# A state-space mixer's output products with operands swapped, and its output turned through DRAM instead of on VectorE

## The chip, the cores and the metric

The kernel runs on one core of a Trainium2 chip. The metric is the time of one execution on the device in microseconds, the median of the runs. The engines are TensorE (PE; PEld is its weight load), VectorE (DVE), ScalarE (ACT), GpSimd (POOL) and SyncE (SP); SP, ACT and POOL also issue transfers, which 16 DMA engines carry out.

## What is computed

A decoder trunk of two layers over 256 tokens of width 2048 in float32. Layer 0 mixes tokens with a gated spatial unit, layer 1 with an S5 state-space layer; each layer then has a SwiGLU block and a gated per-layer embedding. The change lies in layer 1's mixer:

```python
u = (h @ w_in).astype(f32)                       # 256 x 2048
lam_bar = jnp.exp(lam * dt)                      # 128 groups x 64 complex states
bu = lax.complex(...)                            # group input (16 channels) into 64 states
_, s = lax.associative_scan(_lin_combine, (a, bu), axis=1)
y = (jnp.einsum('blgp,gcp->blgc', jnp.real(s), c_re.astype(f32))
     - jnp.einsum('blgp,gcp->blgc', jnp.imag(s), c_im.astype(f32)))
y = y.reshape(bsz, seq, S5_WIDTH) + d.astype(f32) * u
g = jax.nn.gelu(y).astype(h.dtype)
val, gate = jnp.split(g @ w_out, 2, axis=-1)
return val * jax.nn.sigmoid(gate)
```

## The kernel before

All large products go through a stream of 792 weight tiles of 256 x 512 numbers (`ORDER`, tile index t). SP loads tile t into a ring of four buffers (`RAW`), ACT rounds it to its high part (`WHI`, L717), DVE subtracts to get the low part (`WLO`, L976), and PE multiplies with twelve matmuls of 512 columns (high x high, high x low, low x high: L1385 to L1387). ACT's high part of tile t waits until PE has finished tile t-4. The order on every engine is written out by hand: on ACT and DVE, `until(W0 + g)` brings the splitting up to tile W0 + g + 2, and then come the other works of step g. W0 is the first tile of stage `win` (product with `s5_w_in`, 32 tiles); then comes `out1` (product with `s5_w_out`).

Between these tiles lies the S5 core. The sequence of 256 tokens is cut into 32 chunks (NC) of 8 tokens (T). A duo d (8 of them) is 16 groups of 16 channels, two blocks of 128 channels. `turn_u` and `u_chunks` bring u out of token order into `UC` (PE, then DVE, L1282); ACT stores it to the DRAM tensor `ud` and loads it back with channels and in-chunk positions on the partitions as `UP`. `into_states` (L1606, after tile `INTO_AT[d]`) gives the states' inputs, `scan` on DVE (from L1292) runs over the chunks, and `out_of_states` (after tile `OUT_AT[d]`) adds the products with the in-chunk taps `TKK` (L1624) and of the states `SD` with the tables `TD` (L1632). Before `out_of_states` PE waits for the scan, for the tables and for the next `UC`.

The result lies in PSUM with the chunks on the partitions, four strips of 32. `take_y` (ACT, L906) applies GELU and writes `YP`; `turn_y` (DVE, L1315) transposes it in blocks of 32 x 32 into `YG`, which has channels on the partitions; `y_high` (ACT, L913) and `y_low` (DVE, L1320) split that into the high and low parts of the operand `OP` for `out1`. `out1` goes through its first three columns at once: `EARLY` lists them as (column, depth). Column 0 waits for `y_ready` of duo j at depth j; its depths 0 to 7 stand at tiles W0 + 32, 34, 36, 38, 44, 47, 50 and 53.

```python
OUT_AT = [W0 + 8 * (d // 2) + 17 + 2 * (d % 2) for d in range(DUOS - 2)] + [W0 + 42, W0 + 43]
OUT_BANK = [6] * (DUOS - 2) + [4, 4]
Y_AT = [t + 2 for t in OUT_AT]
```

On ACT `take_y(d)` stands at step `OUT_AT[d] + 1` and `y_high(d)` at `Y_AT[d]`; on DVE `turn_y(d)` at `OUT_AT[d] + 2` and `y_low(d)` at `Y_AT[d] + 1`.

Of the kernel before, what the change touches and what calls it, by code (L numbers as in the profile page):

```python
# [6 lines left out]
F32 = mybir.dt.float32  # L7
F32R = mybir.dt.float32r
I32 = mybir.dt.int32
ACT = mybir.ActivationFunctionType  # L10
# [3 lines left out]
P = 128  # L14
# [15 lines left out]
CH = 16  # L30
ST = 64
T = 8
NC = TOK // T
PAIRS = GROUPS // 2
QP = 4
GB = 8
DUOS = KB // 2
DP = 2 * QP
# [34 lines left out]
def end(stage, n):  # L73
    return INDEX[stage, n, DEPTH_OF[stage] - 1] + 1
# [76 lines left out]
W0 = start("win")  # L151
UT_AT = [W0 + 8 * n + 8 for n in range(NT)]
INTO_AT = [W0 + 8 * (d // 2) + 14 + d % 2 for d in range(DUOS)]
OUT_AT = [W0 + 8 * (d // 2) + 17 + 2 * (d % 2) for d in range(DUOS - 2)] + [W0 + 42, W0 + 43]

OUT_BANK = [6] * (DUOS - 2) + [4, 4]
Y_AT = [t + 2 for t in OUT_AT]
DSET = [0, 1, 2, 0, 1, 0, 1, 0]


# [15 lines left out]
def trunk(nc, x, p, norm_mix, norm_ffn, norm_ple, norm_final, gm_w_in, gm_ln_g, gm_ln_b, gm_w_s, gm_b_s,  # L176
# [3 lines left out]
    with ctx:  # L180
        def sem(name):
            return ctx.enter_context(nc.semaphore(name))

        KBYTE = 1024
# [5 lines left out]
        def place(name, shape, dt=F32, at=None):  # L190
            size = 4
            for s in shape[1:]:
                size *= s
            if at is None:
                at = top[0]
                top[0] += (size + 31) // 32 * 32
                assert top[0] <= base + ARENA, name
            return nc.alloc_sbuf_tensor_at(name, shape, dt, offset=at)
# [7 lines left out]
        s_at = top[0]  # L206
# [77 lines left out]
        TD = [f_view(f"TD{i}", [P, 2, QP, 2, P], 16 + 8 * i) for i in range(2)] + [op_view("TD2", [P, 2, QP, 2, P], 8)]  # L284
        TKK = [f_view(f"TK{i}", [P, 2, GB, P], 32 + 8 * i) for i in range(2)] + [op_view("TK2", [P, 2, GB, P], 16)]
# [4 lines left out]
        SD = [op_view(f"SD{i}", [P, 2, DP, NC], 42 + 2 * i) for i in range(2)]  # L290
        RT = [op_view(f"RT{i}", [P, DP, NC], 46 + i) for i in range(2)]
        UC = place("UC", [P, QB, T, NC], at=pt_at)
        UP = [op_view(f"UP{i}", [P, QB, GB, NC], 24 + 4 * i) for i in range(2)]

        YP = place("YP", [P, 2, T, 2, CH], at=s_at)
        YG = place("YG", [P, 2, T, NC], at=s_at + 2 * KBYTE)
        VAL = f_view("VAL", [P, 2, NW], 0)


# [3 lines left out]
        PS = ctx.enter_context(nc.psum_tensor("PS", [P, 8, NW], F32))  # L303
# [3 lines left out]
        tabk = nc.dram_tensor("tabk", (KB, P, T * P), F32).ap()  # L307
        tabe = nc.dram_tensor("tabe", (2, P, PAIRS * NC), F32).ap()
        ud = nc.dram_tensor("ud", (NT, QB, P, T * NC), F32).ap()

        raw_in = [sem(f"raw_in{s}") for s in range(RING)]
        hi_ready = sem("hi_ready")
# [68 lines left out]
        sd_ready = sem("sd_ready")  # L381
        out_of = sem("out_of")
        yp_ready = sem("yp_ready")
        yg_ready = sem("yg_ready")
        y_hi = sem("y_hi")
        y_ready = sem("y_ready")
        g_in = sem("g_in")
# [317 lines left out]
        def _(act):  # L705
            A_ = nc.scalar
# [193 lines left out]

            def take_y(d):
                act.wait_ge(out_of, d + 1)
                if d:
                    act.wait_ge(yg_ready, d)
                for g in range(2):
                    last = A_.activation(YP[:, :, :, g, :].rearrange("p b i c -> p b c i"),  # L906
                                         PS[:, OUT_BANK[d] + g, 0:2 * P].rearrange("p (b c i) -> p b c i", b=2, i=T),
                                         ACT.Gelu_apprx_tanh)
                last.then_inc(yp_ready, 1)

            def y_high(d):
                act.wait_ge(yg_ready, d + 1)
                A_.activation(OP[:, 2 * d:2 * d + 2, 0:TOK].rearrange("p b (k i) -> p b k i", i=T),  # L913
                              YG[:, :, :, :].rearrange("p b i k -> p b k i"), ACT.Copy).then_inc(y_hi, 1)

            for g in range(5, 62):
                until(W0 + g)
                for n in range(NT):
                    if W0 + g == end("win", n):
                        if n:  # L920
                            act.wait_ge(ut_done, 2 * n)
                        take("win", n, in_z, ACT.Copy)
                    if W0 + g == UT_AT[n] + 2:
                        store_u(n)
                    if W0 + g == UT_AT[n] + 4:
                        spread_u(n)
                for d in range(DUOS):
                    if W0 + g == Y_AT[d]:
                        y_high(d)
                    if W0 + g == OUT_AT[d] + 1:  # L930
                        take_y(d)
                if W0 + g == end("out1", 0):
                    act.wait_ge(in_done, DUOS)
                    take("out1", 0, lambda th: VAL[:, th, :], ACT.Copy, scaled=False)
                if W0 + g == end("out1", 1):
                    take("out1", 1, in_s, ACT.Sigmoid, scaled=False)
                if W0 + g == end("out1", 2):
                    act.wait_ge(z_ready, Z_COUNT["out1", 1])
                    take("out1", 2, lambda th: VAL[:, th, :], ACT.Copy, scaled=False)
# [25 lines left out]
        def _(dve):  # L965
            step = Chain(dve, dve_chain)
            V_ = nc.vector
# [57 lines left out]
            for i in range(4):  # L1025
                r = slice(32 * i, 32 * i + 32)
                last = V_.tensor_tensor(IDENT[r, r], IOTA[r, 1, :], IOTA[r, 2, :], ALU.is_equal)
# [142 lines left out]
            for n in (1, 2, 4):  # L1170
                pause()
                last = lambda ri: LP[:, ri, n:n + 1, :].to_broadcast([P, n, PAIRS])
# [18 lines left out]
            for n in range(NT):  # L1191
                f = slice(NW * n, NW * n + NW)
                for th in range(2):
                    last = V_.tensor_scalar(V[:, th, f], V[:, th, f], MV[:, th, 0:1], LNR[:, th, :], ALU.subtract, ALU.mult)  # L1194
# [4 lines left out]
            for n in range(NT):  # L1199
# [5 lines left out]
                for th in range(2):  # L1205
                    for m in range(QB):
                        h = QB * n + m
                        c = slice(P * m, P * m + P)
# [99 lines left out]
                V_.tensor_tensor(SD[d % 2][:, 1, :, 1:NC], part(CV, 1), part(CA, 0), ALU.add).then_inc(sd_ready, 1)  # L1308
                dve.wait_ge(sd_ready, d + 1)

            def turn_y(d):
                dve.wait_ge(yp_ready, d + 1)
                if d:
                    dve.wait_ge(y_ready, d)
                V_.transpose(YG[:, :, :, :].rearrange("p b i k -> p (b i k)"),  # L1315
                             YP[:, :, :, :, :].rearrange("p b i g c -> p (b i g c)")).then_inc(yg_ready, 1)

            def y_low(d):
                dve.wait_ge(y_hi, d + 1)
                V_.tensor_tensor(OP[:, 2 * d:2 * d + 2, TOK:2 * TOK].rearrange("p b (k i) -> p b k i", i=T),  # L1320
                                 YG[:, :, :, :].rearrange("p b i k -> p b k i"),
                                 OP[:, 2 * d:2 * d + 2, 0:TOK].bitcast(F32).rearrange("p b (k i) -> p b k i", i=T),
                                 ALU.subtract).then_inc(y_ready, 1)

            dve.wait_ge(core_ready, 1)
            for g in range(7, 62):
                until(W0 + g)
                for n in range(NT):
                    if W0 + g == UT_AT[n] + 1:
                        u_chunks(n)  # L1330
                for d in range(DUOS):
                    if W0 + g == INTO_AT[d] + 1:
                        scan(d)
                    if W0 + g == Y_AT[d] + 1:
                        y_low(d)
                    if W0 + g == OUT_AT[d] + 2:
                        turn_y(d)
                if W0 + g == end("out1", 1):
                    gated("out1", 1, VAL[:, :, :])
            quad_of("out1", 0, 2)  # L1340
# [25 lines left out]
            f = slice(3 * NW, D)  # L1366
# [6 lines left out]
        def _(pe):  # L1373
# [236 lines left out]
            def out_of_states(d):  # L1610
                n, i, tab = d // 2, d % 2, DSET[d]
                pe.wait_ge(td_in[tab], 32 * (DSET[:d].count(tab) + 1))
                pe.wait_ge(sd_ready, d + 1)
                if d:
                    pe.wait_ge(yp_ready, d)
                pe.wait_ge(uc_ready, 2 * min(n + 2, NT))
                if OUT_BANK[d] == 4:
                    pe.wait_ge(inc_free, DUOS)
                bank = OUT_BANK[d]
                for bl in range(2):  # L1620
                    f = slice(P * bl, P * bl + P)
                    for g in range(2):
                        for q in range(QP):
                            T_.matmul(PS[NC * q:NC * q + NC, bank + g, f], UP[n % 2][:, 2 * i + bl, 2 * q + g, :],  # L1624
                                      TKK[tab][:, bl, 2 * q + g, :], start=(bl == 0), stop=False, skip_group_check=True)
                for bl in range(2):
                    f = slice(P * bl, P * bl + P)
                    for ri in range(2):
                        for q in range(QP):
                            for g in range(2):  # L1630
                                half = slice(ST * g, ST * g + ST)
                                last = T_.matmul(PS[NC * q:NC * q + NC, bank + g, f], SD[i][half, ri, QP * bl + q, :],  # L1632
                                                 TD[tab][half, bl, q, ri, :], start=False, stop=(ri == 1), skip_group_check=True)
                last.then_inc(out_of, 1)

            for t in range(W0, INDEX["out1", 2, 7] + 1):
# [55 lines left out]
```

## Time and profile before

| | |
|---|---|
| time, median of 3 runs (lowest to highest) | 2365.84 us (2365.3 to 2366.28) |
| profiled execution, its own time | 2365.84 us |
| its span, first to last instruction | 2364.1 us |
| mean granted clock of PE | 0.990 |
| busy: PE, DVE, ACT, POOL | 97%, 57%, 44%, 20% |
| weight tiles moved by DMA, mean | 206 GB/s |
| stage of the S5 core | about 1236 to 1390 us |

The page gives each engine's busy time and the chain of work that ended last. As PE is busy nearly all the time, its idle times, its own work and its clock are what makes the length of the kernel. The granted clock is given as a share: 1.00 is 2.4 GHz, 0.50 is 1.2 GHz. Durations of single matmuls overlap, since PE works them in a pipeline: the pace is seen from a burst's length divided by its count.

### The profile page before, as it was taken

The numbers are of one execution on the slowest core, as the hardware profiler recorded it, in microseconds if no ns is written. First come the engines' busy times: TensorE is split into PE (matmuls) and PEld (weight loads), VectorE is DVE, ScalarE is ACT, GpSimd is POOL, SyncE is SP. The second block draws the span as 40 slices with busy tenths as digits, with TensorE's granted clock in tenths as the row PEclk, the third lists the DMA queues.
The fourth block names the chain that finished last, engine by engine and source line by source line (L and its number), as shares of the span: only waits on it lengthen the run. The fifth ranks groups of instructions, "written<-read, shape, count | busy, mean of one in ns | idle before, by whom it ended". The sixth has DMA issues, their size and how long they took to land.

```text
span 2364.1 us, 29152 instructions
## 1 busy us (share of the span) xinstructions
PE 2301.6 (97%) x11853; PEld 1904.2 (81%) x11853; DVE 1336.5 (57%) x1402; ACT 1034.3 (44%) x1252; POOL 474.8 (20%) x438
## 2 busy tenths in 40 slices
PE   5989999999999999999998999999999999999997
PEld 4868888888888888888887788888888888888886
DVE  4786655554555555555656665545445445445565
ACT  3534444444444444444543344444443344444443
POOL 1067304554666355300000000000000000000001
PEclk8999999999999999999999999999999999999999
DMA  6545667766667667666877966566655566665553
GB/s 215 174 152 177 189 194 228 230 216 215 224 219 240 213 217 223 207 214 212 272 245 252 303 212 187 189 192 193 188 187 193 192 193 190 189 190 188 187 205 134
DMA packets 276551, 487.03 MB, mean 206 GB/s; under 512 B 52049, under 2 KB 56545, under 8 KB 276033
## 3 DMA queue, kind: packets, MB, share of 16 engines
q1 hardware_dynamic: 256752, 477.42, 62.6%
q10 hardware_dynamic: 18896, 4.26, 0.8%
q0 software_dynamic: 768, 3.48, 0.4%
q8 instruction: 94, 1.54, 0.3%
q14 instruction: 41, 0.33, 0.0%
HBM read 453.65 MB, written 31.46 MB: 205 GB/s over the span
## 4 chain that ended last, share of the span: by engine, by line
PE 95%; DVE 3%; issue 1%; DMA 1%; ACT 0%; ACTq 0%; SPq 0%; DVEq 0%
PE PS L1385 30%; PE PS L1387 30%; PE PS L1386 30%; PE PS L1414 2%; DVE WLO L976 1%; PE PS L1494 1%; DVE V L1194 1%; PE PS L1632 0%; PE PS L1624 0%; PE PS L1504 0%; PE PS L1606 0%; DMA TE<-tabe 0%; PE PS L1469 0%; DVE OP L995 0%; DVE STAT L1007 0%
## 5 line engine op out<-in xcount | busy, mean ns | idle before, releaser
L976 DVE TENSOR_TENSOR WLO<-RAW,WHI 128x1024 fp32r<-128x1024 f32 x792 | 1038.0, 1314 | 933.0 <-ACT WHI L717 930.9
L1385 PE MATMUL PS<-WHI,OP 128*128 128x512 f32 x3136 | 1235.1, 394 | 27.3 <-DVE WLO L976 27.3
L717 ACT ACTIVATE WHI<-RAW 128x1024 fp32r<-128x1024 f32 x792 | 839.3, 1062 | 941.2 <-PE PS L1387 926.3
L1387 PE MATMUL PS<-WHI,OP 128*128 128x512 f32 x3136 | 1224.0, 390 | 0.0
L1386 PE MATMUL PS<-WLO,OP 128*128 128x512 f32 x3136 | 1223.3, 390 | 0.0
L1385 PEld LDWEIGHTS PS<-WHI,OP 128*128 128x128 f32 x3136 | 590.5, 188 | 154.1 <-issue 33.8
L1387 PEld LDWEIGHTS PS<-WHI,OP 128*128 128x128 f32 x3136 | 590.3, 188 | 124.0
L1386 PEld LDWEIGHTS PS<-WLO,OP 128*128 128x128 f32 x3136 | 591.0, 188 | 119.5
L701 POOL TENSOR_TENSOR ON<-X,GF 128x1024 f32<-128x1024 f32 x3 | 9.9, 3308 | 994.5 <-DVE X L1255 994.5
L640 POOL TENSOR_TENSOR TA<-BRAW,FAC 128x64 f32<-128x64 f32 x16 | 7.1, 445 | 367.3 <-DMA BRAW<-in_s_b_im 367.3
L749 ACT ACTIVATE S<-PS,RC 128x512 f32<-128x512 f32 x68 | 43.1, 685 | 61.9 <-PE PS L1387 61.8
L733 ACT ACTIVATE OP<-PS,VEC 128x256 fp32r<-128x256 f32 x96 | 37.7, 475 | 55.8 <-PE PS L1414 55.8
L995 DVE SCALAR_TENSOR_TENSOR OP<-PS,VEC,OP 128x256 fp32r<-128x256 f32 x96 | 39.7, 477 | 24.5 <-ACT OP L733 24.5
L683 POOL COPY RT<-RHO 128x248 f32<-128x248 f32 x8 | 6.2, 786 | 225.1 <-DVE CB L1299 225.1
L728 ACT ACTIVATE OP<-PS 128x512 fp32r<-128x512 f32 x52 | 28.3, 596 | 52.4 <-PE PS L1414 52.4
L1007 DVE BATCH_NORM_STATS2 STAT<-X 128x6 f32<-128x512 f32 x56 | 35.8, 681 | 0.1
L1244 DVE SCALAR_TENSOR_TENSOR Z<-PS,RC,S 128x512 f32<-128x512 f32 x44 | 31.0, 746 | 7.2 <-PE PS L1387 6.9
L845 ACT ACTIVATE EXP<-PS 128x128 f32<-128x128 f32 (+7 forms) x128 | 17.7, 265 | 39.3 <-PE PS L1504 39.3
L659 POOL TENSOR_TENSOR QT<-TA,TB 128x512 f32<-128x512 f32 x16 | 34.5, 2157 | 1.3
L591 POOL TENSOR_TENSOR V<-V,LG 128x1024 f32<-128x1024 f32 x4 | 11.8, 2959 | 109.7 <-DVE V L1194 109.7
L838 ACT ACTIVATE QS<-PS 128x1024 f32<-128x1024 f32 x16 | 16.4, 1026 | 39.0 <-PE PS L1494 39.0
L989 DVE TENSOR_TENSOR OP<-PS,OP 128x512 fp32r<-128x512 f32 x52 | 33.2, 679 | 0.0
(184 smaller groups left out, 998.3 us busy)
## 6 DMA issues: line engine op xcount, KB each, us to landing
RAW<-in_ffn_w SPq DMA_DIRECT2D x528, 512.0 KB, 4.2
RAW<-in_gm_w_in SPq DMA_DIRECT2D x64, 512.0 KB, 4.3
RAW<-in_ple_w_gate SPq DMA_DIRECT2D x64, 512.0 KB, 4.3
RAW<-in_s_w_out SPq DMA_DIRECT2D x64, 512.0 KB, 4.5
RAW<-in_gm_w_out SPq DMA_DIRECT2D x32, 512.0 KB, 4.1
RAW<-in_s_w_in SPq DMA_DIRECT2D x32, 512.0 KB, 4.8
tabq<-QS SPq DMA_DIRECT2D x16, 512.0 KB, 5.3
tabd<-DT SPq DMA_DIRECT2D x16, 512.0 KB, 6.0
```

The lines of the kernel that those rows point to most:

```text
L659: G_.tensor_tensor(QT[:, :, 1, :, :], TA[:, :, :, :], TB[:, :, :, :], ALU.add).then_inc(q_ready, 1)
L717: A_.activation(WHI[:, t % RING, :], RAW[:, t % RING, :], ACT.Copy).then_inc(hi_ready, 1)
L733: last = A_.activation(OP[:, block_ + 2 * h + m, 0:TOK], PS[:, bank + h, TOK * m:TOK * m + TOK], ACT.Identity, scale=VEC[:, row, k:k + 1])
L749: last = A_.activation(dst(th), acc(stage, n)[:, th, :], func, scale=RC[:, RMS[stage], th:th + 1])
L976: V_.tensor_tensor(WLO[:, t % RING, :], RAW[:, t % RING, :], WHI[:, t % RING, :].bitcast(F32), ALU.subtract).then_inc(lo_ready, 1)
L989: V_.tensor_tensor(OP[:, blocks, TOK:2 * TOK], PS[:, bank + h, :].rearrange("p (k t) -> p k t", t=TOK), OP[:, blocks, 0:TOK].bitcast(F32), ...
L995: last = V_.scalar_tensor_tensor(OP[:, b, TOK:2 * TOK], PS[:, bank + h, TOK * m:TOK * m + TOK], VEC[:, row, k:k + 1], OP[:, b, 0:TOK].bitc ...
L1007: last = V_.bn_stats(STAT[:, th, 6 * n:6 * n + 6], src[:, th, NW * n:NW * n + NW])
L1385: T_.matmul(dst[:, th, :], hi, WHI[:, slot, f], start=begin, stop=False)
L1386: T_.matmul(dst[:, th, :], hi, WLO[:, slot, f], start=False, stop=False)
L1387: last = T_.matmul(dst[:, th, :], lo, WHI[:, slot, f], start=False, stop=finish)
L1414: last = T_.transpose(PS[:, bank + m // 2, at:at + P], src, IDENT[:, :])
```

## The change

In `out_of_states` the two operands of each product are swapped: the table becomes the stationary operand (128 columns of weights), `UP` or `SD` the streamed one (32 columns), and the result has channel and in-chunk position on all 128 partitions and the chunks in the free dimension. `take_y` writes it to one of two `YP` buffers and ACT stores it to a new DRAM tensor `yd` (2048 pieces of 128 bytes for each duo); `gather_y`, four steps later on ACT, loads it back with group and channel on the partitions (256 pieces of 1 KB) into one of two `YG` buffers. The transpose `turn_y` on DVE goes. `y_high` and `y_low` stand six tiles later than before. `YP` and `YG` of one parity share their memory. From the third duo on `take_y` waits for the `y_low` of two duos before.

```diff
...
-Y_AT = [t + 2 for t in OUT_AT]
+YG_AT = [t + 5 for t in OUT_AT]
+Y_AT = [t + 8 for t in OUT_AT]
...
-        YP = place("YP", [P, 2, T, 2, CH], at=s_at)
-        YG = place("YG", [P, 2, T, NC], at=s_at + 2 * KBYTE)
+        YP = [place(f"YP{i}", [P, DP, 2, NC], at=s_at + 2 * KBYTE * i) for i in range(2)]
+        YG = [place(f"YG{i}", [P, 2, T, NC], at=s_at + 2 * KBYTE * i) for i in range(2)]
...
+        yd = nc.dram_tensor("yd", (DUOS, 2 * GB, CH, T, NC), F32).ap()
...
-        yg_ready = sem("yg_ready")
+        yd_in = [sem(f"yd_in{i}") for i in range(2)]
+        yg_in = [sem(f"yg_in{i}") for i in range(2)]
...
             def take_y(d):
...
-                if d:
-                    act.wait_ge(yg_ready, d)
+                if d >= 2:
+                    act.wait_ge(y_ready, d - 1)
                 for g in range(2):
-                    last = A_.activation(YP[:, :, :, g, :].rearrange("p b i c -> p b c i"),
-                                         PS[:, OUT_BANK[d] + g, 0:2 * P].rearrange("p (b c i) -> p b c i", b=2, i=T),
+                    last = A_.activation(YP[d % 2][:, :, g, :], PS[:, OUT_BANK[d] + g, 0:DP * NC].rearrange("p (q k) -> p q k", k=NC),
...
                 last.then_inc(yp_ready, 1)
+                act.wait_ge(yp_ready, d + 1)
+                act.dma_start(yd[d].rearrange("g c i k -> (c i) g k"), YP[d % 2][:, :, :, :].rearrange("p q g k -> p (q g) k")).then_inc(yd_in[d % 2], 16)
+
+            def gather_y(d):
+                act.wait_ge(yd_in[d % 2], 16 * (d // 2 + 1))
+                act.dma_start(YG[d % 2][:, :, :, :].rearrange("p b i k -> p b (i k)"),
+                              yd[d].rearrange("(b g) c i k -> (g c) b (i k)", b=2)).then_inc(yg_in[d % 2], 16)
...
             def y_high(d):
-                act.wait_ge(yg_ready, d + 1)
+                act.wait_ge(yg_in[d % 2], 16 * (d // 2 + 1))
...
-                              YG[:, :, :, :].rearrange("p b i k -> p b k i"), ACT.Copy).then_inc(y_hi, 1)
+                              YG[d % 2][:, :, :, :].rearrange("p b i k -> p b k i"), ACT.Copy).then_inc(y_hi, 1)
...
                         y_high(d)
                     if W0 + g == OUT_AT[d] + 1:
                         take_y(d)
+                    if W0 + g == YG_AT[d]:
+                        gather_y(d)
                 if W0 + g == end("out1", 0):
...
-            def turn_y(d):
-                dve.wait_ge(yp_ready, d + 1)
-                if d:
-                    dve.wait_ge(y_ready, d)
-                V_.transpose(YG[:, :, :, :].rearrange("p b i k -> p (b i k)"),
-                             YP[:, :, :, :, :].rearrange("p b i g c -> p (b i g c)")).then_inc(yg_ready, 1)
-
             def y_low(d):
...
-                                 YG[:, :, :, :].rearrange("p b i k -> p b k i"),
+                                 YG[d % 2][:, :, :, :].rearrange("p b i k -> p b k i"),
...
                     if W0 + g == Y_AT[d] + 1:
                         y_low(d)
-                    if W0 + g == OUT_AT[d] + 2:
-                        turn_y(d)
                 if W0 + g == end("out1", 1):
...
                 bank = OUT_BANK[d]
                 for bl in range(2):
-                    f = slice(P * bl, P * bl + P)
-                    for g in range(2):
-                        for q in range(QP):
-                            T_.matmul(PS[NC * q:NC * q + NC, bank + g, f], UP[n % 2][:, 2 * i + bl, 2 * q + g, :],
-                                      TKK[tab][:, bl, 2 * q + g, :], start=(bl == 0), stop=False, skip_group_check=True)
+                    for q in range(QP):
+                        for g in range(2):
+                            at = NC * (QP * bl + q)
+                            T_.matmul(PS[:, bank + g, at:at + NC], TKK[tab][:, bl, 2 * q + g, :], UP[n % 2][:, 2 * i + bl, 2 * q + g, :],
+                                      start=(at == 0), stop=False, skip_group_check=True)
                 for bl in range(2):
-                    f = slice(P * bl, P * bl + P)
-                    for ri in range(2):
-                        for q in range(QP):
+                    for q in range(QP):
+                        for ri in range(2):
                             for g in range(2):
+                                at = NC * (QP * bl + q)
...
-                                last = T_.matmul(PS[NC * q:NC * q + NC, bank + g, f], SD[i][half, ri, QP * bl + q, :],
-                                                 TD[tab][half, bl, q, ri, :], start=False, stop=(ri == 1), skip_group_check=True)
+                                last = T_.matmul(PS[:, bank + g, at:at + NC], TD[tab][half, bl, q, ri, :], SD[i][half, ri, QP * bl + q, :],
+                                                 start=False, stop=(ri == 1), skip_group_check=True)
                 last.then_inc(out_of, 1)
...
```

## Rows read from the trace of the kernel before

**Rows 1.** the page: busy time of PE, and the chain's shares by engine.

```profile
PE 2301.6 (97%) x11853; PEld 1904.2 (81%) x11853; DVE 1336.5 (57%) x1402; ACT 1034.3 (44%) x1252; POOL 474.8 (20%) x438
...
PE 95%; DVE 3%; issue 1%; DMA 1%; ACT 0%; ACTq 0%; SPq 0%; DVEq 0%
```

**Rows 2.** stretches: busy us (count) by engine, granted clock, DMA share, GB/s.

```profile
1258.00:1262.00 4.00, 4.00 (x100) 3.29 (x93) 0.69 (x1) 2.02 (x3) 0.00 (x0) 0.68 0.94 288
1262.00:1266.00 4.00, 4.00 (x20) 3.27 (x18) 1.85 (x2) 2.09 (x3) 0.00 (x0) 1.00 1.05 399
...
1270.00:1280.00 10.00, 10.00 (x100) 8.34 (x99) 5.79 (x6) 6.08 (x7) 0.00 (x0) 1.00 1.09 336
```

**Rows 3.** chain in order of time, out_of_states: start us, us, what.

```profile
1257.70 1.93 PE PS L1624 x32
1259.64 1.52 PE PS L1632 x64
...
1266.84 1.01 PE PS L1624 x32
1267.85 1.09 PE PS L1632 x64
...
1294.71 1.93 PE PS L1624 x32
1296.64 1.74 PE PS L1632 x64
...
1331.83 1.60 PE PS L1624 x32
1333.43 1.89 PE PS L1632 x64
...
1371.97 1.01 PE PS L1624 x32
1372.98 1.09 PE PS L1632 x64
```

**Rows 4.** waits (us in total, times, longest), and what precedes duo 4.

```profile
PE PS L1624 <- DVE UC L1282: 10.5, 3, 3.8
...
1314.57 2.01 PE PS L1606 x64
...
1316.68 0.69 DVE L1292 TENSOR_TENSOR CA<-PS,TE 128x512 f32<-128x512 f32 x1 [0.28 <-PE PS L1606]
...
1330.40 1.29 DVE UC L1282 x2
```

**Rows 5.** other products: chain's piece, weight loads (min/median/max ns), timeline.

```profile
159.44 1.78 PE PS L1469 x16
...
L1469 PEld LDWEIGHTS PS<-V,WT x64: 188/192/192, 159.0 to 234.4; 128*128 128x128 f32 x64
...
L1606 PEld LDWEIGHTS PS<-UP,TQ x512: 132/138/138, 1240.4 to 1358.3; 128*64 128x64 f32 x171
...
62.87 0.26 PEld L1436 LDWEIGHTS PS<-IDENT,AN 64*128 64x128 f32 x3 [0.35 <-issue]
```

**Rows 6.** groups by line on DVE: busy us, mean ns, idle before.

```profile
L1320 DVE TENSOR_TENSOR OP<-YG,OP 128x512 fp32r<-128x512 f32 x8 | 8.7, 1091 | 0.0
...
L1315 DVE STREAM_TRANSPOSE YG<-YP 128x512 f32<-128x512 f32 x8 | 5.6, 706 | 0.1
```

**Rows 7.** transfers by line: issues, KB each, median us to landing.

```profile
ud<-UC ACTq DMA_DIRECT2D x8, 256.0 KB, 8.5
UP<-ud ACTq DMA_DIRECT2D x8, 256.0 KB, 7.3
```

**Rows 8.** splitting of tiles W0+52, W0+53 (high parts) and W0+53 (low).

```profile
1387.99 1.06 ACT L717 ACTIVATE WHI<-RAW 128x1024 fp32r<-128x1024 f32 x1 [1.66 <-PE PS L1387]
1390.71 1.06 ACT L717 ACTIVATE WHI<-RAW 128x1024 fp32r<-128x1024 f32 x1 [1.66 <-PE PS L1387]
...
1391.80 1.23 DVE L976 TENSOR_TENSOR WLO<-RAW,WHI 128x1024 fp32r<-128x1024 f32 x1 [1.49 <-ACT WHI L717]
```

## The prediction

> **What bounds the kernel now.** I read the page first: TensorE (PE) is busy 97% of the span and makes 95% of the chain that ended last [rows 1]. Time counts only where it is PE's, or where PE waits. The change lies in the "win" and early "out1" columns, some 145 us in which the S5 core is threaded between the weight tiles. So I next read the chain in order of time there, then the waits, then PE, VectorE (DVE) and ScalarE (ACT) in order of time, and last the stretches with the granted clock.
>
> In that stretch `out_of_states` runs eight times, once for each duo d. Undisturbed, it takes 1.01 + 1.09 = 2.10 us; duos 1, 3, 5, 6 and 7 (five bursts) are like this, the first and the last of them shown [rows 3]. Duos 0, 2 and 4 take 1.93 + 1.52, 1.93 + 1.74 and 1.60 + 1.89, in all 10.61 us [rows 3]. Sum of the eight: 10.61 + 5 x 2.10 = 21.1 us. The reason for the slow three: before each of them PE is idle for `UC`, 10.5 us over the three [rows 4], and after the first of them the granted clock reads a mean of 0.68 over four microseconds, much of them at its lower level (1.2 GHz); in the next four it is 1.00 again (2.4 GHz) [rows 2]. A slow burst does about 2.1 us of work in 3.5 us, so one such restart costs about 1.4 us before; where more work follows in the burst, the whole slow stretch of about 3.5 us does 1.75 us of work, and costs 1.75 us.
>
> **The change part by part.**
>
> *The products of `out_of_states` (L1624, L1632).* The number of instructions is the same: each fp32 product is two matmuls with a weight load each, 32 + 64 a duo. But the operands swap. Before, 32 columns of weights are loaded and 128 columns are streamed; the groups sit in four column strips (L1624) and in four strips by two row halves (L1632), and so run side by side: 1.01 us / 32 = 32 ns and 1.09 us / 64 = 17 ns from one start to the next [rows 3]. Afterwards, each product loads 128 columns of weights, which fill the width of the array, and streams only 32. There are no column strips left; for L1632 two row halves remain.
>
> For the first 32 the nearest row is the mixer product L1469: the same 128 x 128 weights, 16 of them in 1.78 us, 111 ns apart [rows 5]. It streams 128 columns where the new one streams 32, so this price holds only if the weights set it. The weight loads speak for that: a load lasts 138 ns for 64 columns (L1606) and 192 ns for 128 (L1469), 54 ns for 64 more columns [rows 5], hence by estimate some 108 ns for 128. The lower bound is L1436, whose three loads of 128 columns take 0.26 us in all at 138 ns each, (0.26 - 0.138) / 2 = 61 ns apart [rows 5]; but these are transposes, and their load is also the shorter one. I take 111 ns: 32 x 111 = 3.55 us.
>
> For the 64 with half the rows no row has 128 weight columns on 64 rows of an ordinary product. The nearest is L1606, which streams the same 32 columns and has two parts of the array side by side, 64 weight columns each: 64 in 2.01 us, 31.4 ns [rows 4]. Twice the weight columns give 62.8 ns if the two row halves load side by side as those column halves do. The upper bound is 111 ns (no overlap), the lower 31.4 ns (weights cost nothing more). I take 62.8, since the old L1632, at 17 ns, is faster than the 32 ns of four strips alone, so row halves do run side by side: 64 x 62.8 = 4.02 us.
>
> A burst at full clock then takes 7.57 us. The three after an idle take 7.57 + 1.75 = 9.32. Sum: 5 x 7.57 + 3 x 9.32 = 65.8 us; less 21.1 it is **+44.7 us**, all of it on PE's path, since PE has nothing else to do meanwhile.
>
> The Trainium skill, page "TensorEngine Tiling (Array Packing)", section Performance Considerations, speaks against this change: with a free dimension of 32 on the streamed side it advises swapping stationary and streamed operand and using four column tiles, for up to 4x. The edit undoes just that. By this rule a burst would be 4 x 2.10 = 8.4 us, the eight 5 x 8.4 + 3 x 10.15 = 72.5 us, the whole change 2422.7 us with the stall below. The trace agrees in sign: 32 ns in four strips against 111 ns at full width.
>
> *The idle before duos 0, 2 and 4* stays. In the third, `into_states` ends at 1316.58, DVE starts the scan at 1316.68, and the second `UC` copy ends at 1331.69 [rows 4]; the turn and `y_low` that leave DVE lie ahead of `into_states`, with DVE idle before the scan. I take the other two to be alike: the same calls in the same order, and the first has no turn ahead of it at all. So the 10.5 us are neither shortened nor lengthened.
>
> *`turn_y` goes* (DVE, 8 x 706 ns [rows 6]): 0. DVE's bound stretches are those from `into_states` to `UC`, and no turn lies in them. Without other cover it would be worth 8 x 0.7 = 5.6 us.
>
> *The trip through DRAM.* Each duo adds on ACT's queue a store of 256 KB in pieces of 128 bytes, and a gather of 256 KB in pieces of 1 KB, behind the `ud` stores and `UP` loads of that queue and beside SP's weight tiles and tables. Like transfers take 8.5 us (`ud`) and 7.3 us (`UP`) to land [rows 7]. A tile lasts 2.72 us (1387.99 to 1390.71) [rows 8]. `gather_y` is four steps after `take_y`, which itself waits for its burst, so at least three tiles = 8.2 us lie between burst and gather; three steps more, again 8.2 us, lie ahead of `y_high`. If a landing is late, ACT stands in `gather_y` or `y_high`, and queued behind it are the high parts of the weight tiles, then DVE's low parts, then PE. That has a margin: a high part may start when the tile four back is done and is needed three tiles later, 8.2 us less 1.06 + 1.23 us of work [rows 8], so 5.9 us. Issues and an excess of 1 to 3 us fit in. The transfer engines are full at times (share 1.09 [rows 2]), so a few microseconds more are possible; but the longer bursts give all of them time. The new wait of `take_y` on `y_ready` is for a `y_low` that DVE has at the same step, before the burst ends. I count 0, bounds 0 and +24 (3 us for each duo).
>
> *`y_high` and `y_low` six tiles later.* For duos 0 to 5 and 7 `y_low` is still two or more tiles early. Not for duo 6: its `y_low` stands at step 51, behind the low part of tile W0+53. The high part of that tile can start only when tile W0+49 is done, and tile W0+50 is the one that needs y_ready 7. So PE must wait: in the trace this high part starts at 1390.71, its low part at 1391.80 and ends at 1393.03 [rows 8]; with `y_low` of 1.09 us [rows 6] it is 1394.1. PE would begin tile W0+50 at 1390.4: the last burst ends at 1372.98 + 1.09 = 1374.07 [rows 3], tile W0+44 follows, and six tiles of 2.72 us are 16.3 us [rows 8]. Stall 3.7 us, and as after the idles before, 1.75 us for the lower clock: **+5.4 us**.
>
> Total: 44.7 + 5.4 = 50.1 us. The profiled execution took 2365.84 us (span 2364.1), which is also the median shown, so **2416 us**, slower by 2.1%.
>
> **The rivals.**
>
> *Rows don't overlap.* If the two row halves load one after the other, 64 x 111 = 7.10 us, a burst 10.65, the eight 5 x 10.65 + 3 x 12.4 = 90.5; +69.4 + 5.4 gives 2441 us. For it: nothing here loads such weights in halves. Against it: the 17 ns of L1632.
>
> *The clock.* The new bursts leave most of the array's streaming idle. After an idle the clock may stay at its lower level to the end of the burst: 3 x 15.14 + 5 x 7.57 + 3 x 1.75 = 88.5, in all +72.8, 2439 us. If it also fell in the other five: 8 x 15.14 - 21.1 + 8 x 1.75 + 5.4 = +119, 2485 us. Against it: the 2 us of L1606 with 32 columns run at one pace.
>
> *Cheap weights.* With 61 ns (L1436) and 31.4 ns (L1606) a burst is 3.96 us, the eight 5 x 3.96 + 3 x 5.71 = 36.9: +15.8 + 5.4, 2387 us.
>
> *Not slower: the instruction rate alone sets the price.* If loads hide wholly, all 96 go at the fastest pace in the trace, 17 ns: 1.63 us a burst, 8 x 1.63 + 3 x 1.63 = 17.9, a gain of 3.2 us, with the stall +2.2: 2368 us. It decides when the mean pace is below about 20 ns. Against it: 111 ns for L1469.
>
> *The trip is late.* +24 us on top: 2440 us. For it: the full transfer engines; against it: margins of 8.2 and 5.9 us.
>
> **How the numbers follow.** Chances: forecast 0.47, rows apart 0.18, clock 0.13 (0.05 of it with all bursts), cheap weights 0.12, late trip 0.05, not slower 0.05. The range 2385 to 2446 takes in all but the last clock case and the not slower one, and some of the tails: about 2 in 10 stay out. The forecast's own range, with 111 ns firm and 50 to 75 ns for the halves, is 2409 to 2423. About 0.2% (4.7 us) is what a measurement here can tell from no change: faster 0.02, same 0.04, slower 0.94.
>
> **What would show it.** The first 32 matmuls of a burst in about 3.5 us, the 64 in about 4.0; waits for `UC` still near 10.5 us; a new wait of PE for `y_low` near tile W0+50 of some 3.7 us, once; ACT waiting for `YG` landings a few us without PE behind it; no other new wait of PE. I am wrong if the bursts take under 3 us or over 10, if the clock is low through them, or if PE waits for high or low parts again and again.

## Result and profile after

The changed kernel takes 2458.17 us (median of 4 runs, 2455.98 to 2460.21) against 2366.06 us before (2365.3 to 2366.51): ratio 1.039, 95% interval 1.0371 to 1.0408. It is 92 us slower. I had said 2416, with 2385 to 2446 as the range: the direction was right, the size wrong. The profiled execution took 2457.38 us, its span is 2455.7 us, 91.6 us over the span before.

The chain in order of time, kernel after; L1626 are the 32 matmuls with `UP` (before: L1624), L1634 the 64 with `SD` (before: L1632). These lines answer to [rows 3]:

```profile
1256.72 7.01 PE PS L1626 x32
1263.73 6.97 PE PS L1634 x64
1271.42 0.43 PE PS L1388
...
1279.20 3.49 PE PS L1626 x32
1282.69 6.23 PE PS L1634 x64
...
1316.84 6.31 PE PS L1626 x32
1323.15 6.97 PE PS L1634 x64
...
1448.81 3.49 PE PS L1626 x32
1452.30 5.27 PE PS L1634 x64
1458.29 0.43 PE PS L1388
...
1475.83 1.06 ACT WHI L720
1476.92 1.23 DVE WLO L987
1478.15 0.96 DVE OP L1324
1479.15 0.80 PE PS L1387
1479.95 0.43 PE PS L1388
```

Two prices stand side by side for the same instructions: 3.49 us or about 7.0 us for the 32. And behind a burst the matmuls of the weight tiles are 0.43 us apart where 0.23 is usual. The last five lines are the wait for `y_low` of duo 6 and the slow tile behind it. The stretches say why (start:end, then busy us and count of PE, PEld, DVE, ACT, POOL, then the granted clock, the DMA share and GB/s), to be held against [rows 2]:

```profile
1240.00:1250.00 10.00, 10.00 (x147) 8.60 (x143) 8.23 (x14) 3.40 (x5) 0.92 (x1) 1.00 0.25 68
1250.00:1260.00 10.00, 6.23 (x30) 5.43 (x28) 7.56 (x12) 1.77 (x2) 0.92 (x1) 0.81 0.42 133
1260.00:1270.00 10.00, 10.00 (x78) 9.94 (x77) 0.00 (x0) 0.00 (x0) 0.00 (x0) 0.50 0.73 284
1270.00:1280.00 10.00, 10.00 (x42) 8.19 (x40) 2.45 (x2) 2.78 (x4) 0.00 (x0) 0.67 0.62 123
1280.00:1290.00 10.00, 10.00 (x92) 9.70 (x92) 0.00 (x0) 0.66 (x2) 0.00 (x0) 0.67 0.60 193
1290.00:1300.00 10.00, 10.00 (x51) 7.84 (x51) 3.67 (x3) 3.50 (x4) 0.00 (x0) 0.81 0.80 207
```

PE is busy all the time and DVE and ACT stand still, but the clock is 0.50 (1.2 GHz) through the first burst and most of the tiles behind it. The second burst, at 1279.20, starts at full clock and loses it while it runs, with no idle of PE in these 10 us or the 10 before. Before, 1262 to 1266 was at 1.00 again. Over the whole stage, 1236 to 1490 us, the granted clock is 0.78 where it was 0.98.

Where the 91.6 us are: the eight bursts last 38.4 us (L1626) and 53.2 us (L1634), 91.6 in all against 21.1 before, +70.5. The tiles behind them run at half clock for 3 to 6 us each time (from 1270.7 to 1276.9 behind the first); about half of that is lost, by estimate some 16 us over the eight. The wait for `y_low` is 3.4 us, and the tiles behind it run at half clock from 1479.2 to about 1484.9, which costs some 3 us more. The waits for `UC` are 11.3 us where they were 10.5:

```profile
PE PS L1626 <- DVE UC L1293: 11.3, 3, 3.8
...
PE PS L1387 <- DVE OP L1324: 3.4, 1, 3.4
```

These (waits: us in total, times, longest) are all of PE's waits of any size in the stage. The sum is 70.5 + 16 + 3.4 + 3 + 0.8 = 94 us against the 91.6 measured; 1 us of the rest is that the first burst starts 1 us earlier than before (1256.72 against 1257.70), and the losses behind the bursts are estimates.

### The profile page after: what moved, and what is told of

Same layout as the page of the kernel before. It is cut to its first block, busy times and chain, and to the rows that moved or that the text cites. A ratio compares the mean times of both kernels' runs of the same rounds, so it can differ in the third digit from the quotient of the medians.

```text
span 2455.7 us, 29152 instructions
## 1 busy us (share of the span) xinstructions
PE 2390.7 (97%) x11853; PEld 1992.5 (81%) x11853; DVE 1314.3 (54%) x1394; ACT 1032.4 (42%) x1252; POOL 487.9 (20%) x438
## 4 chain that ended last, share of the span: by engine, by line
PE 95%; DVE 3%; issue 1%; ACT 0%; DMA 0%; ACTq 0%; DVEq 0%
PE PS L1387 29%; PE PS L1388 29%; PE PS L1389 29%; PE PS L1634 2%; PE PS L1416 2%; PE PS L1626 2%; DVE WLO L987 1%; PE PS L1496 1%; DVE V L1205 0%; PE PS L1608 0%; PE PS L1506 0%; DVE CB L1310 0%; PE PS L1471 0%; DVE OP L1006 0%; DVE STAT L1018 0%
## 5 line engine op out<-in xcount | busy, mean ns | idle before, releaser
L987 DVE TENSOR_TENSOR WLO<-RAW,WHI 128x1024 fp32r<-128x1024 f32 x792 | 1020.9, 1293 | 1041.0 <-ACT WHI L720 1039.2
L1634 PE MATMUL PS<-SD,TD 64*128 64x32 f32 x512 | 53.8, 386 | 0.0
L1634 PEld LDWEIGHTS PS<-SD,TD 64*128 64x128 f32 x512 | 52.7, 315 | 0.4
L909 ACT ACTIVATE YP<-PS 128x256 f32<-128x256 f32 x16 | 5.3, 381 | 110.4 <-PE PS L1634 110.4
L1626 PE MATMUL PS<-UP,TK 128*128 128x32 f32 x256 | 39.2, 321 | 11.3 <-DVE UC L1293 11.3
L1626 PEld LDWEIGHTS PS<-UP,TK 128*128 128x128 f32 x256 | 39.2, 243 | 12.9 <-issue 12.5
```

The source lines that it names most:

```text
L987: V_.tensor_tensor(WLO[:, t % RING, :], RAW[:, t % RING, :], WHI[:, t % RING, :].bitcast(F32), ALU.subtract).then_inc(lo_ready, 1)
L1626: T_.matmul(PS[:, bank + g, at:at + NC], TKK[tab][:, bl, 2 * q + g, :], UP[n % 2][:, 2 * i + bl, 2 * q + g, :], start=(at == 0), stop=Fals ...
L1634: last = T_.matmul(PS[:, bank + g, at:at + NC], TD[tab][half, bl, q, ri, :], SD[i][half, ri, QP * bl + q, :], start=False, stop=(ri == 1), ...
```

## Experiments

The times of before in the same sessions were 2365.9 to 2366.4 us. Ratios are to it, with 95% intervals.

**1. The old products in the changed kernel.** It answers what the trip and the later `y` steps cost by themselves.

```diff
+ T_.matmul(PS[NC * q:NC * q + NC, bank + g, f], UP[...], TKK[tab][:, bl, 2 * q + g, :], ...)
+ T_.matmul(PS[NC * q:NC * q + NC, bank + g, f], SD[i][half, ...], TD[tab][half, bl, q, ri, :], ...)
```

> The changed kernel with the products of out_of_states as they were before (32 columns of weights, 128 streamed); the trip through DRAM, the missing transpose and the later y steps stay. The layout of the products no longer fits what is stored, so the output is not that of the reference; the work is the same. Clock theory (nearly all of the +92 us is the price of the swapped products and the lower clock that goes with them): 2366 + 3.4 + 1.6 for the one wait on y_low = 2371 us, bursts of 2.1 us, clock back to 0.99. Rival, the trip through DRAM costs: each duo's store and gather hold up the high parts of the tiles, and more than 10 us of the 92 remain, 2376 us or more.

Measured 2384.04 us, ratio 1.0072 (1.0057 to 1.0087). So 74 of the 92 us go with the products, but the trip is not free here. The timeline of ACT shows how:

```profile
1264.24 10.96 ACTq L901 DMA_DIRECT2D UP<-ud  x2
1275.24 0.66 ACT L909 ACTIVATE YP<-PS 128x256 f32<-128x256 f32 x2 [11.24 <-issue]
```

The same issues in the changed kernel:

```profile
1276.23 1.90 ACTq L901 DMA_DIRECT2D UP<-ud  x2
```

ACT is held for 11 us by the issue of the two `UP` loads (L901), and `take_y` and all high parts stand behind it. Why it is held so long is not shown: the `yd` store stands ahead of these loads on ACT's queue in the changed kernel too, and without any `yd` store the same pair took 5.1 us in experiment 10. It comes again at 7.2 and 8.4 us behind the next two `ud` stores. PE waits longer for `UC`, and newly for low parts:

```profile
PE PS L1626 <- DVE UC L1293: 15.7, 3, 8.1
...
PE PS L1387 <- DVE WLO L987: 3.6, 3, 3.2
```

The rival's "more than 10 us of the 92" was right for a kernel with short bursts.

**2. The swap alone, in the kernel before.**

```diff
- T_.matmul(PS[NC * q:NC * q + NC, bank + g, f], UP[...], TKK[tab][:, bl, 2 * q + g, :], ...)
+ T_.matmul(PS[:, bank + g, at:at + NC], TKK[tab][:, bl, 2 * q + g, :], UP[...], ...)
  (and the same for SD and TD)
```

> The kernel before with the swapped products alone (128 columns of weights, 32 streamed); the transpose on VectorE and the early y steps stay, so the output is not that of the reference, the work is the same. Clock theory: 2458 less the 5 us of the y_low wait = 2453 us, with the same bursts of 10 to 14 us at a granted clock near 0.5. Rival, trip: under 2440 us, since part of the 92 us is the trip's.

2451.06 us, ratio 1.036 (1.0344 to 1.0375): +85 us. The rest of the change adds only 7 us on top, though experiment 1 gives it 18 alone. Of the 7 us, the wait for `y_low` and the slow tiles behind it are some 6. So the long bursts cover nearly all of the trip.

**3. Four times as much streamed.** This one tells the clock from the weights.

```diff
+WIDE = 4
...
-T_.matmul(PS[:, bank + g, at:at + NC], TKK[tab][:, bl, 2 * q + g, :], UP[n % 2][:, 2 * i + bl, 2 * q + g, :],
+T_.matmul(PS[:, bank + g, at:at + WIDE * NC], TKK[tab][:, bl, 2 * q + g, :], UP[n % 2][:, 2 * i + bl, 0:WIDE, :],
...
-last = T_.matmul(PS[:, bank + g, at:at + NC], TD[tab][half, bl, q, ri, :], SD[i][half, ri, QP * bl + q, :],
+last = T_.matmul(PS[:, bank + g, at:at + WIDE * NC], TD[tab][half, bl, q, ri, :], SD[i][half, ri, QP * bl:QP * bl + WIDE, :],
...
```

> The changed kernel with 128 columns streamed in place of 32 in each swapped product (the same weight loads and count of instructions; more of UP and SD is read, so the output is not that of the reference). Clock theory (the clock falls because little is streamed per weight load): the paces at full clock stay as they are, 109 ns for the first 32 and 54 ns for the next 64, since 128 streamed columns took 111 ns in the spatial product; the clock reads 1.00 through the bursts but for the three behind an idle; bursts 5 x 7.0 + 3 x 8.7 = 61 us in place of 92, no slow tiles behind them: about 2366 + 40 + 5 = 2411 us, faster than the changed kernel although four times as much is streamed. Rival, weights: wide weight loads at this pace lower the clock whatever is streamed, 2458 us, clock 0.5 in the bursts. Rival, streaming: four times as much streaming adds time, over 2458 us.

2413.6 us, ratio 1.02 (1.0183 to 1.0217). Four times as many columns streamed, and 44.6 us *faster* than the changed kernel. Chain and stretches (the edit moves the two lines to L1627 and L1635):

```profile
1271.09 3.57 PE PS L1627 x32
1274.66 3.77 PE PS L1635 x64
```

```profile
1270.00:1280.00 10.00, 10.00 (x108) 9.31 (x107) 0.78 (x1) 1.02 (x3) 0.00 (x0) 1.00 0.93 282
1280.00:1290.00 10.00, 10.00 (x100) 8.30 (x99) 4.75 (x5) 3.88 (x4) 0.00 (x0) 1.00 0.91 249
```

The warm bursts (those that start at full clock) take 7.34 us and the clock stays at 1.00. Streaming 128 columns costs hardly more than 32 (112 and 59 ns a matmul, where 32 columns at full clock have 109 ns, and 58 in experiment 5), so it isn't the streaming that sets the pace, and the weight loads are what is left. And the clock stays up with the same loads at the same pace: only the number of columns streamed to each was changed.

**4. Twice as much streamed** (the same edit with `WIDE = 2`).

> The changed kernel with 64 columns streamed in each swapped product (32 in the changed kernel, 128 in the run before; more of UP and SD is read, so the output is not that of the reference). Clock theory, what counts is how much is streamed beside the weight loads: paces at full clock stay 109 and 54 ns, and the time lies between 2413.6 us (128 columns, clock 1.00) and 2458 us (32 columns, clock 0.5 in the bursts); nearer to 2414 if the first 32, now with half the pace in streaming, no longer lower the clock. Rival: only the length of a product counts, and 64 columns, which last as long as 32 in the records (222 and 223 ns), give 2458 us.

2432.74 us, ratio 1.0278 (1.0261 to 1.0295), between the two. It splits by where a burst starts:

```profile
1258.27 7.06 PE PS L1627 x32
1265.33 7.02 PE PS L1635 x64
...
1279.14 3.52 PE PS L1627 x32
1282.66 3.72 PE PS L1635 x64
```

The three bursts behind an idle stay at the lower clock to their end; the five that start at full clock keep it. With 32 columns neither holds, with 128 both are well (those behind an idle recover within the burst: 5.14 + 3.77 us for the first).

**5. Each burst cut in two,** a weight tile between the halves (`states_part(d)` at tile `OUT_AT[d] + 1`, the last duo one tile later).

> The changed kernel with each burst cut in two: the 32 matmuls with UP after their tile, the 64 with SD after the next tile (the last duo one tile later, so that the two do not meet). The same instructions in the same order, with 2.7 us of full matmuls between. Clock theory: a burst of 3.5 us that starts at full clock ran through at 109 ns a matmul (3.49 us in duos 1, 3 and 7), and the clock fell only behind it; if the tile between is enough to keep it up, the five warm bursts cost 7.0 us each and no slow tiles follow: 2366 + 5 x 4.9 + 3 x about 6 + 5 = 2414 us. If the tile is not enough, 2445 to 2460 us. Rival, weights: the price belongs to the instructions, 2458 us.

2434.04 us, ratio 1.029 (1.0274 to 1.0305): 24 us less than the changed kernel for the same instructions, 20 more than expected if the tile between were enough. Three stretches of its trace:

```profile
1260.00:1270.00 10.00, 10.00 (x47) 8.89 (x46) 0.00 (x0) 0.13 (x1) 0.00 (x0) 0.59 0.90 338
1270.00:1280.00 10.00, 10.00 (x108) 9.42 (x107) 2.36 (x2) 2.67 (x4) 0.00 (x0) 1.00 0.55 104
1390.00:1400.00 10.00, 10.00 (x84) 8.26 (x83) 2.36 (x2) 3.37 (x5) 0.00 (x0) 0.78 0.45 113
```

Most second halves run in 3.69 us, but behind an idle the first half still takes 6.8 to 7.0 us, and some others lose the clock for a while.

**6. The products laid between the long matmuls.**

```diff
  T_.matmul(dst[:, th, :], hi, WHI[:, slot, f], start=begin, stop=False)
+ weave(2)
...
```

`weave(2)` sets the next two products of `out_of_states` (four matmuls), and stands after each matmul of the tile.

> The changed kernel with the swapped products laid two at a time between the matmuls of the two weight tiles that follow, in place of one burst (odd duos one tile later, the last one tile later). The same instructions. Clock theory: there is always a 512-column matmul near, the clock stays at 1.00, and the products cost at most their 7.0 us at full clock for each duo, 56 us less the 21 of before, plus 5 for y_low: 2366 + 40 = 2406 us, less if the weight loads hide behind the long matmuls. Rival, weights or number of instructions: the price is the same wherever they stand, 2458 us. Rival, switching between the shapes of the array costs time at each switch: above 2458 us.

2537.95 us, ratio 1.0726 (1.071 to 1.0742), the slowest of all: my expectation failed by 132 us. PE in order of time:

```profile
1264.68 0.77 PE L1393 MATMUL PS<-WHI,OP 128*128 128x512 f32 x1
1265.25 0.90 PE L1634 MATMUL PS<-UP,TK 128*128 128x32 f32 x4
1265.96 0.77 PE L1395 MATMUL PS<-WLO,OP 128*128 128x512 f32 x1
...
1269.24 0.64 PE L1638 MATMUL PS<-SD,TD 64*128 64x32 f32 x4
1269.81 0.79 PE L1395 MATMUL PS<-WLO,OP 128*128 128x512 f32 x1
1270.53 0.64 PE L1638 MATMUL PS<-SD,TD 64*128 64x32 f32 x4
```

A group of four of the 64 (L1638) and a long matmul take 1.29 us (1269.24 to 1270.53); a group of four of the 32 (L1634, all 128 rows) and a long one take 1.28 us (1264.68 to 1265.96). The stretch they lie in:

```profile
1260.00:1270.00 10.00, 10.00 (x41) 8.41 (x40) 0.00 (x0) 0.00 (x0) 0.00 (x0) 0.50 0.75 290
```

At that clock a long matmul is 0.43 us. Four on half the rows take 0.86, 215 ns each, where they take 109 in a burst; four on all rows take 0.85, 213 ns each, where they take 219 in a burst. So only those on half the rows got dearer. I infer that a product on the upper rows and one on the lower rows no longer run side by side once a full-width matmul stands before and after each pair. That the change between the two shapes costs this time by itself is not ruled out: no run tells the two apart. The long matmuls don't lift the clock from 0.50 either. So neither the clock nor the weights' price is cured by mixing, and the rival on switching was the nearer one.

**7, 8. One half of the swap at a time,** in the kernel before.

> The kernel before with the operands of the 32 matmuls with UP swapped, the 64 with SD as they were (the layouts of the two no longer fit each other, so the output is not that of the reference; the work is the same). Clock theory: a warm burst is 3.49 + 1.09 = 4.6 us, short enough that the clock stays up: 5 x 2.5 = 12 us more; the three behind an idle stay low, 7.0 + 1.5 us in place of 3.5, 15 us more, with some slow tiles behind them: 2393 to 2400 us. Rival, the price is 85 us shared by the count of instructions whatever precedes them: a third, 2394 us, but with the clock low in all eight bursts.

> The kernel before with the operands of the 64 matmuls with SD swapped, the 32 with UP as they were (output not that of the reference, same work). Clock theory: warm bursts 1.01 + 3.5 = 4.5 us at full clock, 5 x 2.4 = 12 us more; behind an idle 1.9 + 7.0 in place of 3.5, 16 us more, and slow tiles behind these, about 9 us: 2403 us. This and the run with the other half swapped then together add less (60 to 70 us) than the 85 us of both swapped, since a burst of half the length doesn't lower the clock. Rival, weights alone: the two parts add up to 85 us, so 2366 + 57 = 2423 us or so here.

The 32 alone: 2404.08 us, ratio 1.0161 (1.0148 to 1.0175). The 64 alone: 2404.96 us, 1.0164 (1.015 to 1.0178). +37.8 and +38.7, in all 76.5 us against 85 for both: less than the sum, as expected, but by 8 us and not by 20. The time of the 32 alone is 4 us over the expected range, that of the 64 alone 2 us over the expected 2403. The chain of the two, first the 32 alone, then the 64 alone:

```profile
1271.53 4.03 PE PS L1624 x32
1275.55 1.89 PE PS L1632 x64
...
1320.05 3.49 PE PS L1624 x32
1323.54 1.08 PE PS L1632 x64
```

```profile
1275.74 1.01 PE PS L1624 x32
1276.75 3.69 PE PS L1632 x64
```

With the 32 alone, three of the five warm bursts still end at the lower clock (such as 4.03 + 1.89) and two don't (3.49 + 1.08); with the 64 alone four of five keep it throughout. So "short enough that the clock stays up" failed for the first, and this pair says less about the clock than experiments 3 to 5.

**9. `y` of duo 6 one step earlier** (`Y_AT[6] -= 1`), in the changed kernel.

> The changed kernel with y_high and y_low of duo 6 one step earlier, and nothing else. If the wait before tile W0+50 is what the step count says (y_low behind the low part of tile W0+53), it shrinks from 3.4 us to about 0.7 us, and with the lower clock behind it some 4 us go: 2454 us. Rival, the wait is the transfers': YG lands too late for the earlier step, and the time stays at 2458 us.

2452.79 us, ratio 1.0365 (1.035 to 1.0381; changed kernel 1.0371 to 1.0408). The wait, 3.4 us in the changed kernel, is now

```profile
PE PS L1388 <- DVE OP L1325: 0.7, 1, 0.7
```

as the count of steps says. The intervals of the ratios overlap a little, so the shorter wait is shown, and not its exact worth in time.

**10, 11. The idle for `UC` in the kernel before.** Duos 0 to 5 two tiles later (`19 + 2 * (d % 2)` in `OUT_AT`), then one tile later (18).

> The kernel before with out_of_states of duos 0 to 5, and take_y, turn_y, y_high and y_low with them, two tiles later, and nothing else. PE was idle 10.5 us before duos 0, 2 and 4 because the UC copy was not done. With two tiles (5.4 us) more it is done in time: the 10.5 us go, and the lower clock in the three bursts behind, 3 x 1.4 us: 2366 - 15 = 2351 us, faster than both kernels. Rival: the idle moves to the next wait on VectorE or on take_y, 2362 us or more.

> The kernel before with out_of_states and what follows it of duos 0 to 5 one tile later (two tiles later put take_y of duo 0 behind the load of UP on the same step of ScalarE, and PE waited 17.1 us for it). One tile later take_y stands a step ahead of that load again. Theory: 2.7 us of each wait for UC (3.8, 2.9, 3.8 us) goes, 8 us in all, and the shorter idle of about 1 us leaves the clock up, 3 x 1.4 us more: 2354 us, faster than both kernels. Rival: a transfer or take_y is next to be late, 2364 us or more.

2384.23 us, ratio 1.0074 (1.0059 to 1.0089), and 2367.95 us, ratio 1.0007 (0.9998 to 1.0016): one slower, one no change. Both expectations failed, and the rivals on record with them (the idle moves to `take_y` or a transfer) came about. PE's waits, first two tiles later, then one:

```profile
PE PS L1624 <- ACT YP L906: 17.1, 3, 6.9
...
PE PS L1624 <- DMA TK<-tabk: 5.1, 1, 5.1
```

```profile
PE PS L1624 <- DVE UC L1282: 9.7, 3, 5.1
PE PS L1385 <- DVE WLO L976: 2.4, 3, 1.6
```

Two tiles later, `take_y` of the even duos falls on ACT's step of `spread_u`, behind its wait for `ud` and its issue, and PE waits for `YP` in place of `UC`. One tile later the chain runs through the `ud` store and the issue of the `UP` loads (start, us, what):

```profile
1258.23 10.01 DMA ud<-UC
1268.26 3.53 ACTq L898
```

I infer that the idle for `UC` had hidden them; no run isolates it. No version was found that beats the kernel before.

## Why the prediction was wrong

*The pace at full clock: right.* 111 ns for the 32 was measured as 3.49 us / 32 = 109 ns; 62.8 ns for the 64 as 3.69 us / 64 = 58 ns (experiments 5, 8). A burst at full clock is 7.2 us, where I had 7.57. The 64 at about half the time of the 32 for each fit row halves that load side by side, and "rows don't overlap" and "cheap weights" fall. Experiment 3 speaks for the weight loads as what sets this pace, since four times the columns change it little. With the clock up there, the whole comes out at 2413.6 us, 2 us from my 2416: the rest of the sum was sound.

*The step that failed* is "a burst at full clock then takes 7.57 us. The three after an idle take 7.57 + 1.75 = 9.32". The swapped burst doesn't keep the clock. The three behind an idle run at 1.2 GHz to their end, but for some 0.7 us at the start of the second (13.3 to 14.0 us), the other five lose it on the way (8.8 to 10.9 us), and the tiles behind, which I had at nothing, pay too. I had this as the rival "the clock", with 0.13, and set against it that L1606 streams 32 columns at one pace. That row was no evidence: it streams its 32 columns every 31 ns, L1626 every 109 ns. The whole-clock rival (2485 us) was too dear, the half-way one (2439) too cheap: by estimate from their lengths at either level, bursts that start at full clock run their first 3 to 5 us at it. That the clock and not the instructions made the difference is shown by experiments 3 and 4, with 5 for the same instructions.

The Trainium skill, page "TensorE: Matmul & The Clock Gate", section "Part 1: The HAM clock gate", says that the array's clock is throttled by default and that activity releases it. The rows agree in this: with more streamed to each load the clock stayed at 1.00 (experiment 3) where it fell with 32 columns. The page puts the fall of the clock down to idle of the engine; here PE shows no idle from 1270 to 1290 (10.00 of 10.00 us busy, twice), and the second burst's pace still fell to that of the lower clock (6.23 us for the 64).

*The idle for `UC`: right* (11.3 us against 10.5, none saved). *`turn_y` at nothing: right*; experiment 2 keeps the turn, and its waits for `UC` are 11.3 us as well.

*The trip at nothing: right in this kernel, for the reason "the longer bursts give all of them time".* The old products show what the cover is worth: 18 us over the kernel before, less about 5 for the `y_low` wait, leaves 13 us. My bound of +24 us held. That an issue could hold ACT for 11 us, I hadn't named.

*The wait for duo 6: right,* 3.4 us against 3.7, at the place that was named. The tiles behind it do run slow for a while, some 3 us where I had 1.75. Taken together, the rest of the change is 7 us over the swap alone (2458.17 against 2451.06), where I had 5.4.

*The clock sum, as it should have been:* bursts 91.6 in place of 65.8 us (+26), slow tiles behind them some 16 us in place of none. Together 42 us, which is what the forecast lacks (2458 - 2416 = 42); the other terms are off by a microsecond or two that cancel.

Open: why the clock in experiment 6 stays at 0.50 beside long matmuls, and why of bursts of 4.6 us (experiment 7) some lose it and some don't.

## What to carry over

Swapping the operands of a small product so that the wide one is loaded and the narrow one streamed turns weight loads into the price: 109 ns a matmul with 128 columns of weights where four strips of 32 side by side took 32 ns. Add to this what it does to the clock: I take the granted clock of a row as evidence for a new stretch only if the row has the same weight loads with as little streamed between them. And a cost that lies hidden in a slowed kernel (here the trip, 13 us) comes back once the slow part is mended, so it should be priced with the cover gone.

## What the hardware showed unexpectedly

PE can be at 1.2 GHz while the page calls it busy throughout, and more streaming to the same weight loads made this kernel faster: 2432.74 us with twice the columns and 2413.6 us with four times, against 2458.17 us. Putting short products between long ones doubled the price of those on half the rows, from 109 to 215 ns each at the lower clock, and left those on all rows as they were. A pair of load issues on ACT took 1.9 us in one schedule and 11.0 us in another, in the same order on the same queue; the cause is open.
